# Product-key choice from all 256 sums instead of 64, turned two tiles later, with operands in PSUM, in a decoder layer on one core

## What is computed

```python
va, ia = lax.top_k(sc[:, :, 0], 16)          # per token and head (8 heads): best 16 of 128 keys, side a
vb, ib = lax.top_k(sc[:, :, 1], 16)          # the same for side b
cand = (va[..., :, None] + vb[..., None, :]).reshape(n_tok, 8, 256)
top, flat = lax.top_k(cand, 16)              # best 16 of the 256 sums
expert = take(ia, flat // 16) * 128 + take(ib, flat % 16)
gate = softmax(top)
out = sum_k gate_k * gelu(w_down[expert_k] . x) * w_up[expert_k]     # 128 experts per token
```

## Time and profile before

| what | us |
|---|---|
| median of 3 runs | 1678.34 (1678.11 to 1678.65) |
| the profiled execution's own time | 1678.76 |
| its span, first to last instruction | 1676.9 |
| PE busy | 1557.5 (93%) |
| DVE busy | 1218.1 (73%) |
| POOL busy | 787.0 (47%) |
| ACT busy | 626.2 (37%) |
| down phase, first to last Gelu | 504.13 to 1133.87 |

### The profile page before, as it was taken

The page is one execution under the profiler, slowest core; times in us unless marked ns, Lnnn a source line. Parts: engine busy times, 40 slices in busy tenths (PEclk is TensorE's granted clock), DMA queues, the critical chain, the costliest instruction groups (busy, mean ns, idle before and its releaser), DMA issues.

```text
span 1676.9 us, 22738 instructions
## 1 busy us (share of the span) xinstructions
PE 1557.5 (93%) x8252; PEld 1387.2 (83%) x8252; DVE 1218.1 (73%) x2298; ACT 626.2 (37%) x807; POOL 787.0 (47%) x460
## 2 busy tenths in 40 slices
PE   7999979897999879996999699999999999999995
PEld 6787857675889879996999699998888888888884
DVE  2544270416999988887988797468888888888887
ACT  4223232322224326632663366333333333333331
POOL 7443454041345777777768777852222222222220
PEclk9999989897999889998999899999999999999997
DMA  8422222113225768797779777998999999999992
GB/s 290 172 95 80 100 101 91 35 50 151 89 75 177 241 213 270 245 390 301 266 243 406 296 254 262 371 364 319 345 334 345 334 339 337 336 342 331 346 379 85
DMA packets 140232, 410.80 MB, mean 245 GB/s; under 512 B 15200, under 2 KB 49248, under 8 KB 139616
## 3 DMA queue, kind: packets, MB, share of 16 engines
q1 hardware_dynamic: 97072, 253.86, 43.1%
q0 software_dynamic: 36864, 134.23, 22.4%
q10 hardware_dynamic: 6192, 21.32, 3.3%
HBM read 363.22 MB, written 46.14 MB: 244 GB/s over the span
## 4 chain that ended last, share of the span: by engine, by line
PE 56%; DVE 17%; DMA 2%; issue 1%; POOL 0%; ACT 0%; DVEq 0%; ACTq 0%
PE ps L1239 10%; PE ps L1241 10%; PE ps L1240 10%; PE ps L927 7%; PE ps L928 7%; PE ps L929 7%; DVE rows L1259 2%; DMA rows<-in_w_down,expert 2%; PE ps L1211 1%; PE ps L1213 1%; DVE gmat L650 1%; DVE gmat L643 1%; DVE ab L733 1%; DVE gb L724 1%; DVE gmat L644 1%
## 5 line engine op out<-in xcount | busy, mean ns | idle before, releaser
L1119 ACT ACTIVATE w_hi<-raw 128x1024 fp32r<-128x1024 f32 x252 | 266.3, 1057 | 346.3 <-PE ps L1241 322.3
L927 PE MATMUL ps<-b_hi,w_hi 128*128 128x384 f32 x1024 | 349.2, 341 | 8.0 <-POOL w_lo L1086 8.0
L1086 POOL TENSOR_TENSOR w_lo<-raw,w_hi 128x1024 fp32r<-128x1024 f32 x119 | 287.9, 2421 | 121.4 <-ACT w_hi L1119 120.4
L928 PE MATMUL ps<-b_lo,w_hi 128*128 128x384 f32 x1024 | 344.6, 337 | 0.0
L929 PE MATMUL ps<-b_hi,w_lo 128*128 128x384 f32 x1024 | 344.5, 336 | 0.0
L1094 POOL DMA_INDIRECT rows<-in_w_up,expert x128 | 139.3, 1088 | 388.4 <-DVE ps L1293 370.9
L1239 PE MATMUL ps<-w_hi,b_hi 128*128 128x512 f32 x768 | 298.8, 389 | 0.7 <-ACT act_t L1125 0.7
L1241 PE MATMUL ps<-w_hi,b_lo 128*128 128x512 f32 x768 | 298.8, 389 | 0.0
L1240 PE MATMUL ps<-w_lo,b_hi 128*128 128x512 f32 x768 | 298.8, 389 | 0.0
L183 POOL TENSOR_TENSOR w_lo<-raw,w_hi 128x1024 fp32r<-128x1024 f32 x60 | 152.0, 2544 | 202.0 <-ACT w_hi L211 202.0
L1300 DVE TENSOR_TENSOR w_lo<-raw,w_hi 128x1024 fp32r<-128x1024 f32 x133 | 163.0, 1225 | 87.8 <-ACT w_hi L1119 87.8
(11 more groups left out here) (217 smaller groups left out, 2467.8 us busy)
## 6 DMA issues: line engine op xcount, KB each, us to landing
raw<-in_down_t SPq DMA_DIRECT2D x128, 512.0 KB, 4.0
raw<-in_up_t SPq DMA_DIRECT2D x128, 512.0 KB, 5.2
raw<-in_units SPq DMA_DIRECT2D x76, 512.0 KB, 3.2
act_d<-act_t SPq DMA_DIRECT2D x128, 192.0 KB, 5.2
c<-act_d SPq DMA_DIRECT2D x128, 192.0 KB, 5.4
gate_d<-gmat ACTq DMA_DIRECT2D x32, 512.0 KB, 15.1
v<-gate_d SPq DMA_DIRECT2D x16, 512.0 KB, 6.7
i<-gate_d SPq DMA_DIRECT2D x16, 512.0 KB, 6.5
```

The costliest lines, as they stand in the source:

```text
L927: nc.tensor.matmul(out, ring.w_hi[:, s, w], b_hi[:, c, 0:DT], start=c == 0, stop=False)
L928: nc.tensor.matmul(out, ring.w_hi[:, s, w], b_lo[:, c, 0:DT], start=False, stop=False)
L1086: nc.gpsimd.tensor_tensor(w_lo[:, s, :], raw[:, s, :], w_hi[:, s, :].bitcast(F32), ALU.subtract).then_inc(split_done, 1)
L1119: nc.scalar.activation(w_hi[:, u % W4, :], raw[:, u % W4, :], ACT.Copy).then_inc(hi_done, 1)
```

## The change

Five edits. (a) `top_experts` makes all 256 sums with one addition into `c0`, and takes max, max_index and match_replace over 256 columns; the index gives the places by a shift and a mask. (b) The places and the keys' numbers are copied to PSUM bank 5 (`place`, `keys`), which comparison and product read from there; from block 1 on a wait for the last block's gate rounds to be taken out (`bank_free`) stands ahead. (c) `TURN_TILE` is 14, not 12, `LEAD` 11, not 9, and a gather in the blocks stands one step earlier relative to its dot. The 26 dots that are left behind the blocks now share 21 tiles, not 23. (d) The copy that makes `numbers` moves from ahead of the choice for `GB` behind it and its gates. (e) In the first layer norm blocks 0 and 1 stay in banks 0 to 3 until their last instruction, and the low parts of transposed blocks 0 and 1 are made between the norms of blocks 2 and 3.

```diff
+            def layer_norm(u0, full, turn, ready, order, in_bank=(), after=lambda b: None):
+                def banks(b):
+                    return ps[:, 2 * b:2 * b + 2, :]
...
-                        added.up(nc.vector.scalar_tensor_tensor(out=xres[:, b, c], in0=xres[:, b, c], scalar=ALPHA,
+                        added.up(nc.vector.scalar_tensor_tensor(out=ps[:, 2 * b + h, :] if b in in_bank else
+                                                                xres[:, b, c], in0=xres[:, b, c], scalar=ALPHA,
                                                                 in1=ps[:, 2 * b + h, :], op0=ALU.mult, op1=ALU.add))
...
+                    x = banks(b) if b in in_bank else wide(xres[:, b, :])
+                    step.up(nc.vector.scalar_tensor_tensor(out=x, in0=x, scalar=mv[:, b, 0:1],
+                                                           in1=wide(lng[:]), op0=ALU.subtract, op1=ALU.mult))
                     done()
+                    nc.vector.scalar_tensor_tensor(out=wide(xres[:, b, :]), in0=x, scalar=rc[:, b:b + 1],
+                                                   in1=wide(lnb[:]), op0=ALU.mult, op1=ALU.add).then_inc(ready, 1)
+                    after(b)
...
-            layer_norm(U_MIX, ln1_full, 2, x1_ready, LN1_ORDER)
-            for b in range(TB):
+            def x1_low(b):
                 dve.wait_ge(x1_hi, b + 1)
...
+            def x1_lows(b):
+                if b == 2:
+                    x1_low(0)
+                    x1_low(1)
+            layer_norm(U_MIX, ln1_full, 2, x1_ready, LN1_ORDER, in_bank=(0, 1), after=x1_lows)
+            x1_low(2)
+            x1_low(3)
...
-    for i0, i1, js, at in PAIR_ROWS:
-        n = i1 - i0
-        step(nc.vector.tensor_tensor(
-            c0[:, :, at:at + n * js].rearrange("p h (i j) -> p h i j", i=n),
-            vs[:, :, 0, i0:i1].unsqueeze(3).broadcast_to([P, PH, n, js]),
-            vs[:, :, 1, 0:js].unsqueeze(2).broadcast_to([P, PH, n, js]), ALU.add))
+    step(nc.vector.tensor_tensor(c0.rearrange("p h (i j) -> p h i j", i=TOPK),
+                                 vs[:, :, 0, :].unsqueeze(3).broadcast_to(shape),
+                                 vs[:, :, 1, :].unsqueeze(2).broadcast_to(shape), ALU.add))
...
-    step(nc.vector.tensor_single_scalar(fi[:, 0], flat[:], 3, ALU.logical_shift_right))
-    step(nc.vector.tensor_single_scalar(fi[:, 1], flat[:], 2, ALU.logical_shift_right))
-    step(nc.vector.tensor_copy(ff, flat[:]))
+    step(nc.vector.tensor_single_scalar(fi[:, 0], flat[:], 4, ALU.logical_shift_right))
+    step(nc.vector.tensor_single_scalar(fi[:, 1], flat[:], TOPK - 1, ALU.bitwise_and))
     done()
-    step(nc.vector.tensor_copy(fif[:], fi[:]))
...
-    step(nc.vector.tensor_tensor(j, ff, j, ALU.subtract))
+    bank_free()
+    step(nc.vector.tensor_copy(place, fi[:]))
+    step(nc.vector.tensor_copy(keys.rearrange("p h s i -> p (h s) i"),
+                               k["i16"][:, bass.ds(b, 1)].rearrange("p o u i -> p (o u) i")))
     done()
     between()
...
-        step(nc.vector.tensor_tensor(pk[side], fif[:, side].unsqueeze(3).broadcast_to(shape),
+        step(nc.vector.tensor_tensor(pk[side], place[:, side].unsqueeze(3).broadcast_to(shape),
...
-        step(nc.vector.tensor_tensor(pk[side], pk[side], isd[:, :, side, :].unsqueeze(2).broadcast_to(shape), ALU.mult))
+        step(nc.vector.tensor_tensor(pk[side], pk[side], keys[:, :, side, :].unsqueeze(2).broadcast_to(shape), ALU.mult))
...
-LEAD = 9
+LEAD = 11
-TURN_TILE = 12
+TURN_TILE = 14
+PICK_BANK = 5
...
+        k["place"] = ps[:, PICK_BANK, 0:2 * HK].rearrange("p (s h i) -> p s h i", s=2, h=PH)
+        k["keys"] = ps[:, PICK_BANK, 2 * HK:4 * HK].rearrange("p (h s i) -> p h s i", s=2, h=PH)
...
-        gathers = [max(LEAD, dots[m - ROWS] + (2 if dots[m] < tail else 1)) if m >= ROWS else LEAD for m in range(HK)]
+        gathers = [max(LEAD, dots[m - ROWS] + 1) if m >= ROWS else LEAD for m in range(HK)]
...
-            step(nc.vector.tensor_copy(numbers[:], k["iota"][:].unsqueeze(2).broadcast_to([P, P, RJ])))
-            top_experts(nc, step, done, k, GB, lambda: None)
+            top_experts(nc, step, done, k, GB, lambda: None, lambda: None)
...
             gates(nc, step, done, k, gate[:])
+            step(nc.vector.tensor_copy(numbers[:], k["iota"][:].unsqueeze(2).broadcast_to([P, P, RJ])))
...
-                top_experts(nc, step, done, k, b, lambda: dots_until(made[0] + 1))
+                top_experts(nc, step, done, k, b, lambda: dots_until(made[0] + 1),
+                            lambda: dve.wait_ge(half_free, halves * b) if b else None)
```

More of the change, by code:

```diff
@@ L458, in inv_std, with wide @@
                 done()
-            def layer_norm(u0, full, turn, ready, order):
+            def layer_norm(u0, full, turn, ready, order, in_bank=(), after=lambda b: None):
+                def banks(b):
+                    return ps[:, 2 * b:2 * b + 2, :]
+                def wide(x):
+                    return x.rearrange("p (i c) -> p i c", i=2)
                 def statistics(b, ready):
@@ L464, in statistics @@
                     for h in range(2):
-                        step.up(nc.vector.bn_stats(bst[:, 2 * b + h, :], xres[:, b, h * HALF:(h + 1) * HALF]))
+                        step.up(nc.vector.bn_stats(bst[:, 2 * b + h, :], ps[:, 2 * b + h, :] if b in in_bank else
+                                                   xres[:, b, h * HALF:(h + 1) * HALF]))
                 for i, b in enumerate(order):
@@ L650, in top_subkeys, with top_experts @@
         step(nc.vector.max_index(place[:, s, b, 8:16], best[:, s, b, 8:16], rest[:, b, :]))
[L655 to L662, removed]
+def top_experts(nc, step, done, k, b, between, bank_free):
+    top, flat, fi, ab = k["top"], k["flat"], k["fi"], k["ab"]
     c0, c1 = k["c0"], k["c1"]
-    ff, fb = k["ab"][:, 0], k["ab"][:, 1]
-    vs, isd = (x[:, bass.ds(b, 1)].rearrange("p o (h s) i -> p (o h) s i", s=2) for x in (k["v16"], k["i16"]))
+    vs = k["v16"][:, bass.ds(b, 1)].rearrange("p o (h s) i -> p (o h) s i", s=2)
+    place, keys = k["place"], k["keys"]
     shape = [P, PH, TOPK, TOPK]
-    whole0, whole1 = c0, c1
-    c0, c1 = (x.rearrange("p h c -> p (h c)")[:, 0:PH * PAIRS].rearrange("p (h c) -> p h c", h=PH) for x in (c0, c1))
-    for i0, i1, js, at in PAIR_ROWS:
-        n = i1 - i0
-        step(nc.vector.tensor_tensor(
-            c0[:, :, at:at + n * js].rearrange("p h (i j) -> p h i j", i=n),
-            vs[:, :, 0, i0:i1].unsqueeze(3).broadcast_to([P, PH, n, js]),
-            vs[:, :, 1, 0:js].unsqueeze(2).broadcast_to([P, PH, n, js]), ALU.add))
+    step(nc.vector.tensor_tensor(c0.rearrange("p h (i j) -> p h i j", i=TOPK),
+                                 vs[:, :, 0, :].unsqueeze(3).broadcast_to(shape),
+                                 vs[:, :, 1, :].unsqueeze(2).broadcast_to(shape), ALU.add))
     done()
@@ L696, in top_experts @@
     done()
-    step(nc.vector.tensor_single_scalar(fi[:, 0], flat[:], 3, ALU.logical_shift_right))
-    step(nc.vector.tensor_single_scalar(fi[:, 1], flat[:], 2, ALU.logical_shift_right))
-    step(nc.vector.tensor_copy(ff, flat[:]))
+    step(nc.vector.tensor_single_scalar(fi[:, 0], flat[:], 4, ALU.logical_shift_right))
+    step(nc.vector.tensor_single_scalar(fi[:, 1], flat[:], TOPK - 1, ALU.bitwise_and))
     done()
-    step(nc.vector.tensor_copy(fif[:], fi[:]))
[L703 to L711, removed]
-    step(nc.vector.tensor_scalar(fb, i, 8.0, 8.0, ALU.mult, ALU.add))
-    done()
-    step(nc.vector.scalar_tensor_tensor(out=j, in0=i, scalar=24.0, in1=j, op0=ALU.add, op1=ALU.add))
-    step(nc.vector.scalar_tensor_tensor(out=fb, in0=i, scalar=16.0, in1=fb, op0=ALU.mult, op1=ALU.min))
-    done()
-    step(nc.vector.tensor_tensor(j, j, fb, ALU.min))
-    done()
-    step(nc.vector.tensor_tensor(j, ff, j, ALU.subtract))
+    bank_free()
+    step(nc.vector.tensor_copy(place, fi[:]))
+    step(nc.vector.tensor_copy(keys.rearrange("p h s i -> p (h s) i"),
+                               k["i16"][:, bass.ds(b, 1)].rearrange("p o u i -> p (o u) i")))
     done()
     between()
-    pk = [x.rearrange("p h (k i) -> p h k i", k=TOPK) for x in (whole0, whole1)]
+    pk = [x.rearrange("p h (k i) -> p h k i", k=TOPK) for x in (c0, c1)]
     for side in range(2):
-        step(nc.vector.tensor_tensor(pk[side], fif[:, side].unsqueeze(3).broadcast_to(shape),
+        step(nc.vector.tensor_tensor(pk[side], place[:, side].unsqueeze(3).broadcast_to(shape),
                                      k["iota"][:, 0:TOPK].unsqueeze(1).unsqueeze(1).broadcast_to(shape), ALU.is_equal))
```

4 lines of the change are left out of this document (removed).

## The result

The changed kernel took **1690.65 us** (median of 4, 1687.83 to 1692.27) beside 1678.49 before: a ratio of 1.0069, 95% interval 1.0055 to 1.0083. It is slower by 12 us, where the prediction had 1625 and a range that ended at 1643. The profiled execution took 1692.27, its span 1690.5.

What follows compares the result with a forecast made beforehand. PE was taken as the bound except where it waited in the down phase (51.0 us). 51.0 plus 7.0 at the front minus 4.5 of waits left gives 53.5 off 1678.76: 1625 us, range 1618 to 1643.

Steps and rivals of the forecast that it cites:

- The step that failed: Down phase, first gate round: two tiles (8.3) behind the turn suffice, as copy and operands take 3.3 to 5.5.
- 48 gate rounds x 1.0: Down phase, tile 0 to 127: gate rounds add 48.0 us to PE's own time of 578.7.
- a gather for the eighth dot waits some 4 us: POOL during the choice: the slower search delays this gather, yet tile 21 behind it keeps 2 us.
- Front: First layer norm to queries: blocks 0 and 1 in PSUM let queries start near 235.6, gaining 7.0 us (3 to 7.5).
- Choice: Picks in the blocks: longer search, shorter remainder; block 0 takes 46.8 us instead of 53.2, block 1 50.5 instead of 57.4.
- the straight line: Search in the choice: 256 columns cost 0.20 to 0.21 us more per instruction than 64, 8.2 us in all.
- GB's experts: Choice for GB: done at 553.8, leaving a cover of 1.0 us for tile 15's low part.
- four thin covers: Down phase: covers of 0.6 to 2.4 us won't all hold; 4.5 us of waits left, bounds 0 and 9.
- Turns: Turns of the picks: all PE waits go, with covers of 2.4 us in block 0 and 6.7 in blocks 1 and 2.
- The transfers' rival: Blocks 1 and 2: gate stores slow the weight loads, eight tiles each at 4.87 to 5.5 us; 1638 us, chance 0.17.
- Slower: Choice: search so dear it delays ACT and PE, x = 18.7 us more to break even, 1692 at 22; chance 0.03.
- closing test: Forecast is wrong if, among other signs, PE's waits from 500 to the up phase sum to over 10.

Runs made afterwards that it cites:

- The choice alone: Kernel before with only the change's choice (256 sums in one addition, positions and key numbers in PSUM; turn at 12, blocks from step 9): 1663.34 us, ratio 0.9914.
- both rings open: Changed kernel with the turn at step 13 and gate stores one piece a tile over 16 tiles, four row buffers: 1628.55 us, ratio 0.9709.
- stores over 14 tiles: Changed kernel with a fifth buffer for gathered rows, the turn at 13 and 16 gate-store pieces over 14 tiles: 1645.14 us, ratio 0.9791.
- the turn alone: Kernel before with only LEAD = 11 and TURN_TILE = 14, gathers still two steps behind their dots: 1657.26 us, ratio 0.9875.

## Why the prediction was wrong

**The step that failed** is the sentence "The first gate round has two tiles (8.3) instead of four behind the turn; copy and operands take 3.3 to 5.5". It priced one round for latency and took the other fifteen as PE's, 5.15 a tile as in the trace ("48 gate rounds x 1.0" in its sum). But before, DVE had no idle time in a round either: its 5.16 was 3.76 of work and 1.40 of catch, held there because POOL followed PE. In the two other phases that were seen the same low part costs about 2.1 and 2.62. The rows that gave the answer were in the trace of before, `eq_b` at 2.08 and `gb`, of the same shape, at 0.68; the question to it, what a full catch would make of the round, was not asked: 3.76 + 2.62 = 6.38 against 5.16, times 16 rounds and 3 blocks, some 58 us, more than the whole forecast gain. 60.6 were lost. In the changed kernel the start of it is visible in block 0: the rounds began at 609.05, a low part caught each of the first two (2.88 and 3.29), the second ended at 620, four dots held back until then took 4.6 us more, low parts caught the third round once and the fourth twice (3.17 and 3.25), and tile 31 came 4.5 us late. From there the gather waits for the dot and the ring stands.

The sentence on POOL's gathers was part of it: "a gather for the eighth dot waits some 4 us" was looked at inside the choice. That the same earlier gather puts POOL behind the dot in every gate round was not. POOL waited for dots 141.3 us, 57 times, between 495 and 1160 after the change; before, 25.1 us, 17 times.

*The rest, in order.*
- **Front, 7.0 forecast, 3.5 seen** (first Gelu at 500.64, not 504.13); alone, 2.7. The four PSUM instructions took 1.28 to 1.29 each as forecast, and from the first norm to the queries' first matmul it was 21.2 us (215.82 to 237.01) where the earlier trace rows gave 27.7. That gain of 6.5 is the same in all fifteen traces that have the edit (21.2, against 27.6 to 27.7 in the four that don't), so the mechanism held and its size nearly. The rest isn't the edit's: the norm itself began 0.9 later in this execution (it starts anywhere from 211.7 to 216.1 in the nineteen traces), and from the queries' first matmul to the first Gelu it took 263.6 us instead of 261.6, with a mean granted TensorE clock of 0.81 of full speed from 300 to 400 where before had 0.85. The kernel with the turn at 12, which has the same front, had 0.85 there and 261.6 again.
- **Choice.** Search 0.42 for find, 0.41 for max and replace; the straight line through the earlier trace rows was right. GB's exponent fell at 531.97, in the times of before 535.5 (forecast 535.1). Block 0's choice took 45.1 us (46.8 forecast), from 555.89 to 601.0; block 1's took 46.0, from 720.19 to 766.17 (50.5 forecast). The choice alone gained 15 us.
- **GB's experts, 553.8 forecast, 554.66 + 3.5 = 558.2 seen.** The subtraction's catch was counted as gone, "since POOL then has no work". POOL's low parts caught both new shifts instead (2.47 and 2.43 where a free one takes 0.22). The 4.4 ate the cover of 1.0 and PE waited 5.07 for tile 15's low part. Of the four thin covers this one broke, and 4.5 of waits was the forecast for all.
- **Turns.** Covers of blocks 0, 1 and 2 all held: no wait. But they were wider than needed: in block 0 DVE stood 5.0 us waiting for the turned picks, and block 1's picks were ready at 766.2 while the turned ones came at 775.5. The turn at 14 spared PE no wait that 13 had, and took DVE's lead.
- **Rivals.** The transfers' rival named the right crowd, the gate stores, and the wrong victim: weights came late, PE did not wait for low parts, DVE was caught. It priced the stores at 13 us. With the turn at 13 they cost 39, with it at 14 11. Slower was given 3% and one mechanism, a dear search, which did not come. Its closing test, PE's sum of waits over 10, was right to look at PE and not at one place.

The sum with the measured terms in it: 1625.3 + 63.5 (stage) + 3.5 (front) = 1692.3, and the profiled execution took 1692.27. As stage and front were themselves read from the trace, this says only that nothing changed behind the stage. With both rings open, the same forecast stands 3.3 us from the measurement, 1628.55 against 1625.3. That is another kernel than the one predicted, and part of the agreement is luck: its stage took 585.2 where 583.2 was forecast, but of the 6.3 by which its first Gelu came earlier (497.85), 2.1 are a first norm that happened to start earlier.

## What to carry to other kernels

A tile time read off a trace is a steady state of several engines, not a price of one. Before moving a step that another engine queues behind, take each engine's round apart into its own work and what holds it, put every hold at its full length, and see whether the sum passes the bound's pace; if it does, the kernel can have a second state, and lead, buffers and bursts decided here which one it ran in. Keep a tile of slack on both sides of a hand-over rather than moving it as late as its cover allows, and spread a bulk store to the bandwidth that the loads leave.

## What the hardware showed that was not expected

- The catch reaches small instructions too: a shift of 128 elements a partition with one input tensor took 2.47 us instead of 0.22 beside a low part, and a scaling of the same size 2.30 (stores over 14 tiles) and 2.89 (the turn alone) instead of 0.23.
- One kernel's executions differed by over 10 us from one to the next (1639.38 to 1652.77, five buffers and the turn at 13, one chip), with the same program and a granted clock of 0.977 to 0.979 in all four. Small differences can tip it: over 14 tiles of stores block 2 had four late weights (3.7 us in all, the last of them, 2.1, in its first rounds) and lost 9.1 us; over 16 tiles it had two (0.5 in all) and lost 0.4. What separates executions of one kernel stays open.
- A gather's instruction took POOL 0.95 us beside a free DVE, 1.16 to 1.23 in gate rounds, and up to 2.84 beside a choice (the turn at 13).
